# Attention stage of a hybrid encoder step: the routing picks of batches 0 to 2 in four chunks over four steps

## The reference

```
p = rms_norm(x) @ w_in                     # a, gate, q, k, v
c = swish(layer_norm(causal_conv31(a * sigmoid(gate))))
# stick-breaking attention, 8 heads of 64, per block of 128 queries:
z = q @ k.T / 8
log_keep = where(valid, log_sigmoid(-z), 0)
a = where(valid, exp(log_sigmoid(z) + (sum of log_keep over later keys)), 0)
o = rms_norm(a @ v)
x = x + concat(c, o) @ w_out
h = rms_norm(x)
# router: best of 4 groups, then the best two of its 8 experts
lg = h @ w_rg;  g = argmax(lg);  p_sel = softmax(lg)[g]
le = (h @ w_re)[group g];  top_v, top_i = top_k(le, 2)
combine = p_sel * softmax(top_v)
# rows sorted by expert in blocks of 128, then for each block
y += combine * ((silu(h @ w_g[e]) * (h @ w_u[e])) @ w_d[e])
```

## Time and profile before

| | |
|---|---|
| runs, us | 2189.45, 2194.96, 2197.71 |
| profiled execution: its time, us | 2193.86 |
| its span, us | 2192.1 |
| granted PE clock, mean | 0.982 |
| PE busy, us (share of the span) | 2089.6 (95%) |
| DVE busy | 1619.1 (74%) |
| ACT busy | 1259.1 (57%) |
| POOL busy | 767.8 (35%) |
| chain that ended last: PE, DVE | 38%, 1% |

### The profile page before, as it was taken

The page is one execution under the profiler, slowest core; times in us unless marked ns, Lnnn a source line. Parts: engine busy times, 40 slices in busy tenths (PEclk is TensorE's granted clock), DMA queues, the critical chain, the costliest instruction groups (busy, mean ns, idle before and its releaser), DMA issues. The chain is left out here.

```text
span 2192.1 us, 40169 instructions
## 1 busy us (share of the span) xinstructions
PE 2089.6 (95%) x13511; PEld 1762.5 (80%) x13512; DVE 1619.1 (74%) x2084; ACT 1259.1 (57%) x2199; POOL 767.8 (35%) x696
## 2 busy tenths in 40 slices
PE   8999999996899999799999897999999999999998
PEld 6888888884687887678787775888888888888887
DVE  3799999995677667867878967879699556456643
ACT  5322433345677777766676643768687456455533
POOL 1111444553566655545544453112111112111111
PEclk9999999997999999999999998999999999999999
DMA  6563334334433242333222116999899968667851
GB/s 224 190 206 137 119 125 157 132 106 144 125 106 109 80 138 77 106 107 116 80 73 92 54 61 237 373 315 371 299 372 375 311 203 275 219 206 263 287 169 34
DMA packets 211805, 393.17 MB, mean 179 GB/s; under 512 B 54781, under 2 KB 81789, under 8 KB 211677
## 3 DMA queue, kind: packets, MB, share of 16 engines
q1 hardware_dynamic: 198141, 357.42, 47.1%
q0 software_dynamic: 13536, 34.12, 6.6%
HBM read 315.42 MB, written 91.23 MB: 186 GB/s over the span
## 5 line engine op out<-in xcount | busy, mean ns | idle before, releaser
L2122 POOL TENSOR_TENSOR late<-late,p_past 128x1024 f32<-128x1024 f32 (+4 forms) x166 | 308.2, 1857 | 347.6 <-DVE p_past L1979 344.4
L2526 DVE TENSOR_TENSOR p_w_lo<-p_raw,p_w_hi 128x1024 fp32r<-128x1024 f32 (+1 forms) x196 | 330.4, 1720 | 134.0 <-ACT p_w_hi L2318 134.0
L796 DVE SCALAR_TENSOR_TENSOR p_ut<-p_ut,p_cw 128x512 f32<-128x512 f32 (+1 forms) x480 | 329.1, 762 | 0.0
L2318 ACT ACTIVATE p_w_hi<-p_raw 128x2048 fp32r<-128x2048 f32 (+1 forms) x150 | 271.6, 1842 | 62.3 <-PE p_up L2410 53.3
L1979 DVE TENSOR_TENSOR_SCAN p_past<-p_keep,p_past,p_one 128x513 f32<-128x513 f32 (+1 forms) x196 | 225.8, 1192 | 76.5 <-ACT p_keep L1796 74.4
L1796 ACT ACTIVATE p_keep<-p_zp 128x512 f32<-128x512 f32 (+3 forms) x326 | 158.7, 547 | 118.4 <-PE p_zp L1670 105.7
L2410 PE MATMUL p_gp<-p_w_hi,p_xt_hi 128*128 128x256 f32 x736 | 214.0, 291 | 0.0
L473 PE MATMUL p_pj<-p_w_hi,p_xt_hi 128*128 128x512 f32 x512 | 205.4, 401 | 4.2 <-DVE p_xt_lo L772 2.4
L2410 PE MATMUL p_gp<-p_w_hi,p_xt_lo 128*128 128x256 f32 x736 | 206.2, 280 | 0.0
L2410 PE MATMUL p_gp<-p_w_lo,p_xt_hi 128*128 128x256 f32 x736 | 206.2, 280 | 0.0
L473 PE MATMUL p_pj<-p_w_hi,p_xt_lo 128*128 128x512 f32 x512 | 200.8, 392 | 0.0
(11 more groups left out here) (315 smaller groups left out, 5019.8 us busy)
## 6 DMA issues: line engine op xcount, KB each, us to landing
p_raw<-in_w_up SPq DMA_DIRECT2D x96, 512.0 KB
p_raw<-in_w_gate SPq DMA_DIRECT2D x96, 512.0 KB
p_raw<-in_w_down SPq DMA_DIRECT2D x96, 512.0 KB
late<-in_w_up SPq DMA_DIRECT2D x32, 512.0 KB
late<-in_w_gate SPq DMA_DIRECT2D x32, 512.0 KB
late<-in_w_down SPq DMA_DIRECT2D x32, 512.0 KB
wide_raw<-in_w_in SPq DMA_DIRECT2D x56, 256.0 KB, 3.7
wide_raw<-in_x SPq DMA_DIRECT2D x17, 512.0 KB
```

Source lines behind the costliest of these rows:

```text
L796: dve.scalar_tensor_tensor(dst, src, cw[:, a, j:j + 1], dst, ALU.mult, ALU.add).then_inc(tap_done, 1)
L2122: pool.tensor_tensor(mine, mine, past_rows[:, u % NP, 0:n, 2:2 + w], ALU.mult).then_inc(a_done, 1)
L2318: act.activation(part(w_hi, p, wide), ring(n, wide), ACT.Copy).then_inc(whi_done, wide)
L2526: dve.tensor_tensor(part(w_lo, p, wide), ring(n, wide), part(w_hi, p, wide).bitcast(F32), ALU.subtract).then_inc(wlo_done, wide)
```

## The change

The two functions `pick_first` and `pick_second` become four: `pick_group` (best group, 7 instructions, and the cast of the iota for batch 0), `pick_first` (best expert, 6), `pick_second` (second expert, 6) and `choose` (`chosen` and the difference, 2 or 3). For batches whose `pick_step` is at most `end - 8` = 158, which are 0, 1 and 2, they run in the four steps after `pick_step`, one in each. Batches 3 and 4 keep their two steps. No instruction is added, taken out or changed. The planner's cost of a pick on DVE becomes 15 in each of the four steps for these batches, and stays 30 in each of two for the others. By that the second halves of units 119, 137, 151 and 152 are copied by ACT instead of DVE; no other copy changes sides.

```
-            dve += 30 * sum(1 for e in pick_step.values() if e in (s - 1, s - 2))
+            dve += sum(15 for e in pick_step.values() if e <= end - 8 and s - 4 <= e < s)
+            dve += sum(30 for e in pick_step.values() if e > end - 8 and s - 2 <= e < s)
...
-            def pick_first(b):
+            def pick_group(b):
...
                 first_max(n, NG, mine, best[:, 0, 0:n], best[:, 1, 0:n], ohg[:, 0:n, :])
                 link(dve.tensor_tensor(picks.group[:, lo:hi, :], mine, over(best[:, 0, 0:n], n, NG), ALU.subtract))
                 link(dve.tensor_scalar(eq[:, 0:n, :], ohg[:, 0:n, :], BIG, -BIG, ALU.mult, ALU.add))
+
+            def pick_first(b):
+                lo, hi = BATCHES[b]
+                n = hi - lo
                 link(dve.tensor_tensor(cand[:, 0:n, :].rearrange("p t (g e) -> p (t g) e", g=NG),
...
                 first_max(n, NE, cand[:, 0:n, :], best[:, 3, 0:n], picks.expert[:, 1, lo:hi], oh[1][:, 0:n, :])
+
+            def choose(b):
+                lo, hi = BATCHES[b]
+                n = hi - lo
                 end = dve.tensor_tensor(chosen[:, 0:n, :], oh[0][:, 0:n, :], oh[1][:, 0:n, :], ALU.add)
...
+            pick_parts = [pick_group, pick_first, pick_second, choose]
...
-                for b in at_step(pick_step, s - 1):
-                    pick_first(b)
-                for b in at_step(pick_step, s - 2):
-                    pick_second(b)
+                for part, late_part in ((pick_group, 1), (pick_first, 1), (pick_second, 2), (choose, 2)):
+                    for b, e in sorted(pick_step.items()):
+                        if s == e + (late_part if e > end - 8 else pick_parts.index(part) + 1):
+                            part(b)
```

## The result

The changed kernel takes 2197.63 us (median of 12 executions, 2194.43 to 2202.12); the kernel before, timed beside it, 2194.49 (12 executions, 2189.45 to 2197.71). The ratio is 1.0018 with a 95% interval of 1.0011 to 1.0026; a second measurement gave 1.0015 [1.0006, 1.0025]. By the page of the changed kernel its profiled execution has a span of 2195.0 us (2196.75 us in all) at a mean granted clock of 0.982, as before.

What follows compares the result with a forecast made beforehand. The prediction took DVE to bound the kernel at the picks, with PE waiting for it. Batch terms of -0.4, -0.2 and 0 summed to -0.6 us, giving 2193.3 or 2194.4, middle 2193.8 us; range 2184 to 2203.

Steps and rivals of the forecast that it cites:

- The signs that it named for being right: PE gaps near 1065 and 1156 under 1 us, new gaps within 15 us behind, DVE as full as before.
- rival 2: Picks in batches 0 and 1: fewer holds than counted, about -6 us, 2188.5 us; chance 0.15.
- Batch 0: PE's 2.49 us gap goes, but DVE is late again at `p_le`; gain 0.4 us.
- The three holds: Batch 0: `pick_first`, `pick_second` and `choose` wait for POOL's product, 1.30, 0.5 and 0.5 us.
- Batch 1: From `p_m_lo` to the scan of step 142, added holds eat DVE's 1.89 us idle time; gain 0.1 to 0.2 us.
- the low spells: PE's lower clock behind gaps in batches 0 and 1, taken as 1.9 and 2.9 us of work lost.
- Batch 2: Net 1.6 us more of DVE, against 0.83 + 1.16 us idle behind ACT and POOL; gain 0.
- Rival 1: At the picks, PE's gaps and low clock are all won back, 14.4 us, to 2180.5 us; chance 0.15.
- Rival 3: Second and fourth pick steps of each batch: each added chunk held in full, +10.9 us, 2205.9 us; chance 0.10.
- scans escape the holds: DVE's scans name two SBUF tensors yet aren't held: 1.79 us under two products, 1.80 with POOL idle.

Runs made afterwards that it cites:

- before_again: The kernel before, unedited, built and profiled a second time; 2193.76 us, ratio 0.9998.
- before_twice: The kernel before with the second pick's six instructions issued twice in batches 0 to 2; 2198.35 us, ratio 1.0021.
- copies_only: The kernel before, two long picks kept, with only the change's planner costs, so four copies pass from DVE to ACT; 2195.01 us, ratio 1.0002.
- split_b02: The change in batches 0 and 2 alone, batch 1 as in the kernel before; 2195.93 us, ratio 1.0006.
- after_again: The changed kernel, unedited, measured a second time; 2197.74 us, ratio 1.0015 to the kernel before.
- after_look: The changed kernel, unedited, profiled a third time; 2194.70 us in one execution.
- two_psum: The kernel before, two long picks, with the picks' small tiles in PSUM and the difference taken before chosen; 2187.97 us, ratio 0.9965.
- before_fill: The kernel before with 164 unneeded matmuls ahead of four jobs where PE waits; output altered, whole time not comparable; batches 103.10 us, behind them 100.92.
- split_only: The change's four pick chunks with the planner's costs and copies of the kernel before; 2199.19 us, ratio 1.0021.
- after_fill: The changed kernel with 122 unneeded matmuls ahead of six jobs where PE waited; output altered, whole time not comparable; 99.48 us behind the batches.
- after_fill_2: The changed kernel with the matmuls of after_fill, but without the start flag; 2195.55 us, ratio 1.0003 to the kernel before.

## Why the prediction was wrong

The signs that it named for being right came: PE's gaps near 1065 and 1156 are under 1 us, new ones stand behind them, DVE is as full as before. The time still went the other way, a loss of 3 to 4 us for a gain of 0.6. That it lies in the range of 2184 to 2203 says little for the mechanism: the range is 19 us wide and took in rival 2 as well.

**Batch 0: mechanism right, gain 0.4 forecast, 0.1 lost.** DVE's rows of the changed kernel, answering:

```profile
1061.75 1.61 DVE L1901 TENSOR_TENSOR p_cand<-p_le,p_eq 128x128 f32<-128x128 f32 x1
...
1064.68 0.73 DVE L1884 TENSOR_TENSOR p_oh<-p_oh,picks 128x128 f32<-128x128 f32 x1
...
1068.35 0.82 DVE L1909 SCALAR_TENSOR_TENSOR p_cand<-p_oh,p_cand 128x128 f32<-128x128 f32 x1
...
1074.89 0.80 DVE L1916 TENSOR_TENSOR p_chosen<-p_oh 128x128 bf16<-128x128 f32 x1
```

The three holds are 1.32, 0.53 and 0.51 us above the 0.29 of a free instruction; forecast were 1.30, 0.5 and 0.5. What I missed is the second row, 0.73: POOL also normalises the `o` tile behind its product, 0.61 us, and holds the pick that stands there. The kernel before has that row as well:

```profile
1064.54 0.73 DVE L1883 TENSOR_TENSOR p_oh<-p_oh,picks 128x128 f32<-128x128 f32 x1
```

I took 1.94 us for six free instructions and so dropped 0.44 us, which is the gain I forecast. PE's wait of 2.49 us went, and came back as 1.30 at the rank and 1.09 at `p_le`, as the prediction said of an early gain.

**Batch 1: the step that failed.** It was "9.3 against 9.35. The idle time is eaten by holds. Gain 0.1 to 0.2 us." DVE's rows of the changed kernel from `p_m_lo` to the scan of step 142, answering, with the one held instruction ahead of them:

```profile
1146.71 1.53 DVE L1880 TENSOR_TENSOR p_ohg<-p_lg,p_best 128x16 f32<-128x16 f32 x1
...
1152.32 1.38 DVE L1880 TENSOR_TENSOR p_oh<-p_cand,p_best 128x128 f32<-128x128 f32 x1
...
1158.11 0.68 DVE L1946 TENSOR_TENSOR p_m_lo<-p_mp,p_m_hi 128x512 fp32r<-128x512 f32 x1
1158.71 0.50 DVE L1909 SCALAR_TENSOR_TENSOR p_cand<-p_oh,p_cand 128x128 f32<-128x128 f32 x1
...
1160.55 0.75 DVE L1884 TENSOR_TENSOR p_oh<-p_oh,picks 128x128 f32<-128x128 f32 x1
...
1163.47 1.57 DVE L1920 TENSOR_SCALAR p_chosen<-p_chosen,p_valid 128x32 bf16<-128x32 bf16 x1
...
1168.09 2.31 DVE L2015 SCALAR_TENSOR_TENSOR p_h<-wide_raw,p_st,p_g 128x512 f32<-128x512 f32 x1
1170.32 1.79 DVE L1990 TENSOR_TENSOR_SCAN p_past<-p_keep,p_one 128x385 f32<-128x385 f32 x2
```

From `p_m_lo` to that scan are 1170.32 - 1158.11 = 12.21 us. My sum gave 11.8; the 0.4 missing is again the pick held by POOL's normalising (0.75 - 0.29). `p_m_lo` itself stands 2.63 us sooner behind the batch's first route than in before_again (17.92 against 20.55), where I said 2.5. So the sum was good. The other side of the comparison wasn't: in before_again the same way takes 8.30 us, not 9.35:

```profile
1159.56 0.68 DVE L1935 TENSOR_TENSOR p_m_lo<-p_mp,p_m_hi 128x512 fp32r<-128x512 f32 x1
...
1165.51 2.33 DVE L2004 SCALAR_TENSOR_TENSOR p_h<-wide_raw,p_st,p_g 128x512 f32<-128x512 f32 x1
1167.86 1.80 DVE L1979 TENSOR_TENSOR_SCAN p_past<-p_keep,p_one 128x385 f32<-128x385 f32 x2
```

The idle 0.82 + 1.07 us of the earlier trace rows are missing there; 0.9 us of them are a longer hold of `p_h` instead (2.33 against 1.39). They go with a long low spell of PE in batch 1: about 7 us of low clock and 0.82 us of that idle time in the profile on which I predicted and in before_twice; half as long and 0 and 0.34 us in before_again and copies_only; no low clock and 0 in split_b02, where batch 1 isn't split. So they belong to an execution in which PE was late with its bank. I wrote of this spell that it is work lost, and in the same sum spent the idle time that stood behind it. 12.21 - 2.63 - 8.30 = 1.28 us is what batch 1 loses, and the stretches say 34.90 - 33.64 = 1.26.

**The clock: a term that the prediction didn't have.** I priced the low spells as PE's loss (4.8 us) and asked only whether the change wins them back. The rows say something else. A short spell inside a batch is nearly free, because DVE is what PE waits for: batch 0 of the kernel before takes 33.52 us at a clock of 0.95 and 33.52 at 1.00.

```profile
1048.76:1082.28 33.52, 30.79 (x242) 25.24 (x240) 30.98 (x62) 23.06 (x51) 14.56 (x11) 0.95 0.31 102
```

One twice as long cost about 1 us in batch 1 of the kernel before (34.68 against 33.64), and nothing in the change's (34.92 in after_again, 34.90 with the fill). Behind a batch PE is the bound and a spell costs about 1.5 us (57.24 - 55.70, 27.30 - 25.75; 17.45 - 16.27 for a part of one). The long wait of the kernel before stands early in the batch, and its spell has passed when the batch ends: behind its batches all four profiles of unsplit picks in SBUF without a fill (before, before_again, copies_only, before_twice) have 97.68 to 97.76 us. In its own three the change has 98.34 to 99.71. Only in the first of them, though, does the moved wait explain the most of it: the spell behind the wait of 2.07 us runs over the end of batch 1, 1.18 us. In after_again it ends just ahead of it and 0.40 us are left; in after_look the 1.6 us come behind the short wait that all kernels have. The same place has it in two_psum, whose picks aren't split (99.33 behind the batches), and before_fill, without its long early waits, had two spells behind its batches. So a low clock behind the batches is what the change's profiles have more of; that the moved waits bring it is shown in one of three profiles and argued for the rest.

**The account.** Batches: 103.66 (before, before_again, copies_only) to 104.72 (the change's three), in the mean +1.06. Behind: 97.72 to 99.06, +1.34. The rest of the stage up to the last route: 69.57 to 69.11, -0.46, with 68.06 to 70.91 in the six profiles. Together the stage grew by 1.9 us, of the 3.3 to 4.0 measured. Where the other 1.4 to 2.1 us lie stays open; the interval of the ratios (1.3 to 5.7 us) is wide enough for them to be nothing. Shown are the loss, that the split makes it, and 1.26 us of it in batch 1, against an execution of the kernel before without the long low spell.

**Batch 2: right.** Forecast 0, 36.15 against 36.03 and 36.42. `p_chosen` was held in full (2.18 us at 1241.10), and the batch came out no longer. The two copies less weren't needed for that (36.16 in split_only, which has them on DVE), so DVE's wait for POOL's late `p_st` covered it.

**The rivals.** Rival 1 is out: nothing was won back but what DVE set. Rival 2 is out: every hold came. Rival 3 had the right sign and half of the mechanism: the short choosing chunk is held in full in batches 1 and 2, but the price, 1.3 us in one batch, was an eighth of its 10.9. None had the low clock behind the batches.

The prediction says that scans escape the holds although they name two SBUF tensors. That is a misreading of the kernel: `p_one` is declared as `one = ps("one", [P, 4 * P])` and lies in PSUM, so the scan of 1.79 us reads one tensor of SBUF, and it is no exception. The working of the holds stands on the Trainium skill (SBUF — State Buffer, section Who interferes with whom), whose rule I had given as speaking against this change; on that it was right, and two_psum bears it out from the other side (1.53 to 0.18 us with an input in PSUM).

## What to carry to other kernels

Splitting an engine's work to shorten another's wait gained nothing here while the first engine bounded the stretch, and it moved the wait to where that stretch ends; there it can cost more, when the low clock behind it falls on work that TensorE bounds (1.2 us in one profile). Before spending idle time found in a profile, ask what made it, and look at a second execution. Cheaper than moving held instructions was taking away what they are held by: the same picks with one operand in PSUM made the kernel 5.8 and 6.5 us faster in two builds.

## What the runs showed of the hardware

- A DVE instruction of almost no work is held as long as a big one: 32 columns of bf16 with a per-partition scalar from SBUF took 1.57 us under a product of POOL (1163.33 to 1165.01) in the change, and 0.23 us in before_twice, where POOL's product had ended at 1155.72 and the next began at 1162.15.
- A matmul with the start flag, into columns of a PSUM bank that nobody else uses, changes sums that are open in other columns of the same bank: in after_fill the first output moved by 0.38 of its size, and in after_fill_2, the same matmuls at the same places without the flag, it didn't move. The Trainium skill (PSUM — Partial Sum Buffer, section The four PSUM rules) says that such a matmul clears the marks of the whole bank for the partitions that it writes; these runs agree.
- The same kernel's attention stage, from batch 0 to the last route, took 271.65 and 269.36 us in two executions, and the change's 272.04, 272.84 and 273.79; much of it comes in steps of about 1.5 us, one for a low spell that falls where PE is full (55.70 and 57.24, 25.75 and 27.52 us for the same work).
